# A two-block transformer kernel: the first conditioning quarter in two groups, X read first, three blocks open at once, and one reordered step of the attention stage

## What is computed

```python
mod = jax.nn.silu(c) @ w_ada[l] + b_ada[l]
shift1, scale1, gate1, shift2, scale2, gate2 = jnp.split(mod, N_MOD, axis=-1)
h = rms_norm(x, norm1_w[l]) * (1.0 + scale1[:, None]) + shift1[:, None]
proj = h @ w_in[l]
```

## Time and profile before

| | us |
|---|---|
| median of 3 runs | 2520.4 (2519.49 to 2521.88) |
| profiled execution, its own time | 2518.81 |
| span of that execution's trace, first to last instruction | 2516.9 |
| PE busy | 2475.8 (98%) |
| DVE busy | 1970.6 (78%) |
| ACT busy | 1298.0 (52%) |
| mean granted clock of PE, of full speed | 1.0 |

### The profile page before, as it was taken

How to read it: one execution, slowest core, us unless ns; L and a number is a source line. 1 busy time by engine, 2 the same in 40 slices (tenths; PEclk the granted TensorE clock), 3 DMA queues, 4 the chain that set the end, 5 groups by cost and what they waited for, 6 DMA issues and landing times.

```text
span 2516.9 us, 32571 instructions
## 1 busy us (share of the span) xinstructions
PE 2475.8 (98%) x12413; PEld 2089.9 (83%) x12413; DVE 1970.6 (78%) x2318; ACT 1298.0 (52%) x1736; POOL 258.5 (10%) x304
## 2 busy tenths in 40 slices
PE   6999999999999999999999999999999999999999
PEld 5877888878988888888888888888888888888887
DVE  7888988897888998999977687896865566665555
ACT  4544555344554544544545676566554454453553
POOL 1000310000011211111110002452000010010000
PEclk9999999999999999999999999999999999999999
DMA  9998879997899999999967656464576776766654
GB/s 348 339 353 315 290 258 328 369 320 235 297 334 340 324 341 337 322 343 335 339 231 233 184 168 193 148 220 165 192 222 233 233 224 234 226 226 198 188 191 159
DMA packets 299485, 662.87 MB, mean 263 GB/s; under 512 B 20785, under 2 KB 21137, under 8 KB 298561
## 3 DMA queue, kind: packets, MB, share of 16 engines
q1 hardware_dynamic: 296944, 652.31, 76.3%
q0 software_dynamic: 1808, 6.77, 0.8%
q10 hardware_dynamic: 576, 1.70, 0.2%
HBM read 658.61 MB, written 2.10 MB: 263 GB/s over the span
## 4 chain that ended last, share of the span: by engine, by line
PE 78%; DVE 11%; issue 4%; ACT 3%; DMA 3%; POOL 0%; SPq 0%; ACTq 0%; DVEq 0%
PE PS L662 77%; DVE WL L1573 3%; DVE ACC L1581 2%; ACT WH L1150 2%; PE PS L665 1%; DVE UQ L1573 1%; DMA RAWX<-in_w_b_up 1%; DVE A L1967 1%; ACT EX L1150 1%; DVE SM L1584 1%; DMA RAW<-in_w_in 1%; DVE KP L1573 1%; DMA RAW<-in_w_ff 0%; DVE EX L1573 0%; DVE WX L1573 0%
## 5 line engine op out<-in xcount | busy, mean ns | idle before, releaser
L1150 ACT ACTIVATE WH<-RAW 128x1024 fp32r<-128x1024 f32 x569 | 602.1, 1059 | 687.4 <-PE PS L662 524.4
L1573 DVE TENSOR_TENSOR WL<-RAW,WH 128x1024 fp32r<-128x1024 f32 x570 | 705.5, 1239 | 316.3 <-ACT WH L1150 315.0
L662 PE MATMUL PS<-WH,AH 128*128 128x512 f32 x2052 | 809.4, 394 | 6.9 <-DVE WL L1573 3.1
L662 PE MATMUL PS<-WL,AH 128*128 128x512 f32 x2052 | 799.2, 389 | 0.0
L662 PE MATMUL PS<-WH,AL 128*128 128x512 f32 x2052 | 797.8, 390 | 0.0
L662 PE MATMUL PS<-HL,WH 128*128 128x512 f32 (+1 forms) x2176 | 642.0, 383 | 0.8 <-issue 0.6
L662 PEld LDWEIGHTS PS<-WH,AH 128*128 128x128 f32 x2052 | 385.4, 188 | 90.4 <-DVE WL L1573 7.8
L662 PEld LDWEIGHTS PS<-WH,AL 128*128 128x128 f32 x2052 | 385.1, 188 | 81.2 <-DVE AL L1573 0.3
L662 PEld LDWEIGHTS PS<-WL,AH 128*128 128x128 f32 x2052 | 385.6, 188 | 76.7
L662 PEld LDWEIGHTS PS<-HL,WL 128*128 128x128 f32 x2048 | 378.3, 188 | 85.2
L662 PE MATMUL PS<-HL,WL 128*128 128x256 f32 x2048 | 397.7, 278 | 0.0
(11 more groups left out here) (250 smaller groups left out, 1921.1 us busy)
## 6 DMA issues: line engine op xcount, KB each, us to landing
RAW<-in_w_ff SPq DMA_DIRECT2D x334, 512.0 KB, 4.5
RAW<-in_w_ada SPq DMA_DIRECT2D x276, 512.0 KB, 5.3
RAW<-in_w_in SPq DMA_DIRECT2D x194, 512.0 KB, 4.4
RAWX<-in_w_ada SPq DMA_DIRECT2D x108, 512.0 KB, 5.4
RAWY<-in_w_ff SPq DMA_DIRECT2D x96, 512.0 KB, 3.7
RAWX<-in_w_ff SPq DMA_DIRECT2D x82, 512.0 KB, 5.2
RAWX<-in_w_in SPq DMA_DIRECT2D x46, 512.0 KB, 5.2
RAW<-in_w_out SPq DMA_DIRECT2D x32, 512.0 KB, 3.6
```

The source lines that it names most:

```text
L662: return e.matmul(o, l, r, start=start, stop=stop, skip_group_check=True)
L1150: return e.activation(o, i, f, **kw)
L1573: return e.tensor_tensor(o, a, b, op)
```

## The change

1. **Two groups.** The first quarter is cut in two groups of channel tiles, 0 and 1, then 2 and 3. A group is 8 items of a new kind "h": two of the 16 columns of silu(c) at once, 256 channels of shift1 and of scale1 for each. An item is two DMAs with runs of 1 KB (before, one with runs of 2 KB), and DVE accumulates it in two dependent steps over 512 columns.
2. **Order of the stream.** X, the first group, three chunks, the second group, then chunk 3 and on; the second quarter is spread over 17 chunks instead of 20.
3. **Three blocks open.** The first six chunks go in the order (0, 2, 4, 1, 3, 5): channel tiles 0 and 1 of blocks 0, 1, 2, then tiles 2 and 3 of the same. Blocks 1 and 2 are now open for four chunks each.
4. **Turns.** PE does four turns of X ahead of the first sums; turns 4 and 5 after the second sums, ahead of chunk 3; turn 6 ahead of chunk 5 and turn 7 ahead of chunk 6, in banks 6 and 7. ACT copies them at its steps 2, 6 and 7.
5. **Orders.** DVE does 8 items, the first modulation, WL and AL for it, WL of two more chunks, then the 8 items of the second group, its modulation, WL of chunk 3 and AL. keep_on is 4 and 12 products around the first sums (before 10 and 9), and 5 between turns 4 and 5.
6. **Attention ahead of rotary.** In DVE's `side`, dilated stands before rope.

```diff
+HEAD_FIRST = (0, 2, 4, 1, 3, 5)
 def sum_parts(q):
-    return ((0, 1), (1, 4)) if q == 0 else ((0, 4),)
+    return ((0, 2), (2, 4)) if q == 0 else ((0, 4),)
...
+    early = [[("h", (part, m), v[:, 2 * m:2 * m + 2, 0:2, part * 256:(part + 1) * 256]) for m in range(8)] for part in range(2)]
...
-    plan += quarter[0]
+    head = [head[c] for c in HEAD_FIRST] + head[6:]
+    plan += early[0] + head[:3] + early[1]
...
-        a, n = 20 * (q - 1), 20
+        a, n = (3, 17) if q == 1 else (20 * (q - 1), 20)
...
-            out.append(("in1" if c1 == 8 else "part", n, at, c1 - c0))
+            first, ticks = (at // 2, 4) if at in (2, 4) else (at, c1 - c0)
+            out.append(("in1" if c1 == 8 else "part", n, first, ticks))
...
-                if i == 1:
+                if i == 0:
                     e.dma_start(X[:, :, :], I["x"][0].rearrange("(t p) d -> p t d", p=128)).then_inc(s_x, 16)
...
+                if kind == "h":
+                    dst = dst.rearrange("p (t g n) -> p t g n", t=2, g=2)
+                    for t in range(2):
+                        e.dma_start(dst[:, t], src[:, t]).then_inc(s_raw[st.slot[i]], 16)
+                    continue
...
-            for i in range(8):
-                b = 4 + i % 3
+            def first_turn(i):
+                b = 4 + i % 3 if i < 4 else 6 + i % 2
...
+                if i == 5:
+                    e.wait_ge(s_mod, 6)
+                elif i > 2:
+                    e.wait_ge(s_xT, (1, 3, 0, 5, 6)[i - 3])
...
+            for i in range(4):
+                first_turn(i)
+            def early(part):
+                k0, k1 = sum_parts(0)[part]
+                e.wait_ge(s_ada, st.group_last["q", 0, part][1])
+                for k in range(k0, k1):
+                    for g in range(2):
+                        at = 512 * part + 256 * g + 128 * (k - k0)
+                        m = mm(PS[:, 7, 4 * g + k:4 * g + k + 1], ACC[:, at:at + 128], ones[:, 0:1], True, True)
+                m.then_inc(s_sum, 1)
...
             for j in range(AUP):
                 if j == 0:
-                    keep_on(3, 10)
-                if j in SUMS:
+                    keep_on(3, 4)
+                    early(0)
+                    keep_on(3, 12)
+                elif j in SUMS:
                     quarter(SUMS.index(j))
-                if j == 0:
-                    keep_on(3, 9)
+                if j == 3:
+                    early(1)
+                    first_turn(4)
+                    e.wait_ge(s_mod, 6)
+                    keep_on(7, 5)
+                    first_turn(5)
+                if j in (5, 6):
+                    first_turn(j + 1)
...
                 if j == 0:
                     feed(0)
-                    for k0, k1 in sum_parts(0):
-                        quarter(0, k0, k1)
+                    quarter(0, 0, 2)
                 if j not in norms:
                     feed(j + look(j))
+                if j == 1:
+                    quarter(0, 2, 4)
+                if j == 2:
+                    first_copy(4)
+                    first_copy(5)
+                if j in (6, 7):
+                    first_copy(j)
...
+                    if m == 0:
+                        if part == 0:
+                            e.wait_ge(s_cs, 2)
+                        ts(acc, row[:, 0, :], CS[:, 0:1], None, ALU.mult, None).then_inc(s_ada, 1)
+                    else:
+                        e.wait_ge(s_ada, st.ada[i] - 2)
+                        stt(acc, row[:, 0, :], CS[:, 2 * m:2 * m + 1], acc, ALU.mult, ALU.add).then_inc(s_ada, 1)
+                    e.wait_ge(s_ada, st.ada[i] - 1)
+                    stt(acc, row[:, 1, :], CS[:, 2 * m + 1:2 * m + 2], acc, ALU.mult, ALU.add).then_inc(s_ada, 1)
...
+                for h, s in due(p, DIL0, 8, 2, (2, 4)):
+                    dilated(h, s)
                 for r, s in due(j, ROPE0, 8, 4, (0, 4)):
                     rope(r, s)
-                for h, s in due(p, DIL0, 8, 2, (2, 4)):
-                    dilated(h, s)
...
-            for i in range(5):
+            for i in range(3):
                 item(i)
...
-            for i in range(5, 7):
+            for i in range(3, 5):
                 item(i)
...
-            for i in range(7, 16):
+            for i in range(5, 8):
                 item(i)
...
                     quarter(0)
                     feed(0)
-                    quarter_low(0, 0, 1)
+                    quarter_low(0, 0, 2)
...
+                    if j == 1:
+                        while done[0] < st.group_last["q", 0, 1][0]:
+                            item(done[0])
+                            done[0] += 1
+                        quarter(0, (1,))
                     feed(j + ahead(j))
+                    if j == 1:
+                        quarter_low(0, 1, 2)
```

More of the change, by code:

```diff
@@ L233, in __init__ @@
             age[s] = i
-            uses[s] += 1
+            uses[s] += 2 if kind == "h" else 1
             self.slot[i], self.land[i], self.before[i] = s, 16 * uses[s], held[s]
@@ L241, in __init__ @@
             else:
-                ada += 1
+                ada += 2 if kind == "h" else 1
                 self.ada[i] = ada
@@ L249, in __init__ @@
                     self.group_last["q", info[0]] = (j - 1, ada)
+                if kind == "h" and info[1] == 7:
+                    self.group_last["q", 0, info[0]] = (i + 1, ada)
         self.raw_x_done = [max([self.j[i] + 1 for i in range(n) if self.slot[i] > 3 and self.j[i] < 434
@@ L361, in __init__ @@
         for n, c0, c1 in PIECES:
-            q = self.first if n == 0 else self.starts[len(self.head)]
+            at = len(self.head)
+            q = self.first if n == 0 else self.starts[at // 2 if at in (2, 4) else at]
             self.head += [(q, c, c == c0 and (n > 0 or c == 0), c == c1 - 1) for c in range(c0, c1)]
+        self.head = [self.head[c] for c in HEAD_FIRST] + self.head[6:]
     def both(self, q):
@@ L647, in _ @@
                 dst = raw_at(i)
-                if kind != "a":
+                if kind == "h":
[3 more added lines that the diff above has]
+                    continue
+                elif kind != "a":
                     dst = dst.rearrange("p (t n) -> p t n", t=2)
@@ L758, in _ @@
                     e.wait_ge(s_dg, 2)
-                if i > 2:
-                    e.wait_ge(s_xT, i - 2)
+                if i == 5:
+                    e.wait_ge(s_mod, 6)
+                elif i > 2:
+                    e.wait_ge(s_xT, (1, 3, 0, 5, 6)[i - 3])
                 for k in (2 * i, 2 * i + 1):
@@ L771, in quarter @@
                 e.wait_ge(s_xT, 8)
[L772 to L786, removed]
+                e.wait_ge(s_mod, 3 * summed(q, 0) - 3)
+                for g in range(2):
+                    for k in range(4):
+                        at = 1024 * (q % 2) + 512 * g + 128 * k
+                        m = turn(PS[:, 6 + g, 128 * k:128 * k + 128], ACC[:, at:at + 128])
+                m.then_inc(s_sum, 1)
             def ada_turn(b, g, n):
@@ L1192, in _, with first_copy @@
             af(SM[:, 0:1], vc("q_norm_w"), ACT.Copy, scale=INV_SQRT).then_inc(s_vc, 1)
-            for i in range(8):
+            def first_copy(i):
                 e.wait_ge(s_xnT, i + 1)
-                af(xT[:, 2 * i:2 * i + 2, :].rearrange("p a s -> p (a s)"), PS[:, 4 + i % 3, :], ACT.Copy).then_inc(s_xT, 1)
+                b = 4 + i % 3 if i < 4 else 6 + i % 2
+                af(xT[:, 2 * i:2 * i + 2, :].rearrange("p a s -> p (a s)"), PS[:, b, :], ACT.Copy).then_inc(s_xT, 1)
+            for i in range(4):
+                first_copy(i)
             def quarter(q, k0, k1):
-                e.wait_ge(s_mod, 3 * summed(q, 0 if q or k1 == 1 else 1))
+                e.wait_ge(s_mod, 3 * summed(q, 0 if q or k1 == 2 else 1))
                 for k in range(4 * q + k0, 4 * q + k1):
@@ L1608, in item @@
                     return
+                if kind == "h":
+                    part, m = info
+                    acc = ACC[:, 512 * part:512 * part + 512]
+                    row = raw_at(i).rearrange("p (t n) -> p t n", t=2)
+                    if m == 0:
[7 more added lines that the diff above has]
+                    stt(acc, row[:, 1, :], CS[:, 2 * m + 1:2 * m + 2], acc, ALU.mult, ALU.add).then_inc(s_ada, 1)
+                    return
                 blk, g, t, h = info
@@ L1636, in feed, with quarter @@
                     done[0] += 1
-            def quarter(q):
-                for part, (k0, k1) in enumerate(sum_parts(q)):
+            def quarter(q, parts=(0,)):
+                for part in parts:
+                    k0, k1 = sum_parts(q)[part]
                     cols_q = slice(4 * q + k0, 4 * q + k1)
@@ L1648, in quarter @@
                             continue
-                        tt(MOD[:, row, cols_q], PS[:, 6 + (k0 > 0), 4 * g + k0:4 * g + k1], bias, ALU.add).then_inc(s_mod, 1)
```

(5 more changed lines are left out.)

## The result

The changed kernel took **2527.49 us** (median of 10 runs, 2525.96 to 2530.06) against 2519.42 for the kernel before (10 runs, 2517.22 to 2521.88): ratio **1.0032**, 95% interval 1.0024 to 1.0040. It is slower by some 8 us. The prediction was 2528.0, in a range of 2523 to 2531.5. The profiled execution took 2527.05 us; its span is 2525.2, against 2516.9 before: 8.3 more.

What follows compares the result with a forecast made beforehand. PE bounds the kernel, busy 2475.8 of 2516.9 us, so only its pauses move. Terms 7.2 + 1.8 + 0.75 - 2.3 = +7.5 us on the profiled 2518.8 give 2526.3, median 2528; range 2523 to 2531.5.

Steps and rivals of the forecast that it cites:

- First group: Start of the kernel: first turn at 20.35 us, modulation at 28.7, chunk 0 at 31.45, 6.4 us earlier than before.
- Narrower accumulation: DVE's conditioning items: two dependent 512-column steps, 0.85 us each with the gap, make a group of eight take 13.3 us.
- Second group and pause: DVE finishes at 47.9 us, PE pauses from 39.6 to 48.0 and resumes at half rate; chunk 3 at 54.4, +7.2.
- The rival that the clock stays up: PE's pause: clock stays at 2.4 GHz, chunk 3 at 52.0, sum +5.1, 2525.5 us; chance 0.15.
- Behind it: Stream after chunk 3: turns 6 and 7 between chunks add 1.8 us, late reading of a bank 0.75.
- the late bank: Chunk 6: PE waits for the bank of block n=1, which ACT reads late; +0.75 us, ends 0 and 1.35.
- Swap: Attention ahead of rotary on DVE near 1655 us: PE's waits for KP and EX both go, -2.3 us.
- the second rival: Later stages absorb up to 4 of the 4.7 us PE waits for WL: sum +3.5, 2523.9 us; chance 0.13.

Runs made afterwards that it cites:

- keep_through: The changed kernel with 32 more keep-on products between chunk 2 and the second group's sums, filling PE's pause: 2526.30 us, ratio 1.0016.
- no_swap: The changed kernel with the old order of the rotary and attention steps restored: 2528.51 us, ratio 1.0032.
- dve_two: The changed kernel with DVE accumulating items 11 and 12 of the second group ahead of the first modulation, loads unmoved: 2528.13 us, ratio 1.0028.
- x_second: The changed kernel with X loaded behind item 0, as in the kernel before: 2528.74 us, ratio 1.0036.
- ada_moved: The changed kernel with six conditioning items moved from chunks 96 to 108 of the stream to chunks 50 to 76: 2526.73 us, ratio 1.0034.
- combo2: The changed kernel with two second-group items loaded and accumulated early, turns 4 to 7 and keep-on products in PE's pause: 2522.11 us, ratio 1.0009.
- turns_in_pause: The changed kernel with turns 4 to 7 and ACT's copies of them moved into PE's pause behind chunk 2: 2524.24 us, ratio 1.0016.

## Why the prediction was right

- **First group: right.** ACT began on X at 9.92 (predicted 9.6), the first turn was at 20.69 (20.35), the first modulation at 28.85 (28.7), chunk 0 at 31.28 (31.45), the idle time of DVE there.
- **Narrower accumulation: right to 4%.** The step of 512 columns took 0.75 us, eight took 6.46, or 0.82 from start to start (predicted 0.74 and 0.85). The group took 12.8 us, predicted 13.3. The Trainium skill, VectorE: DVE Perf Modes, section The DRAIN you can't avoid, says that a semaphore after each step of a chain costs nothing extra; the estimate that I worked out from that was 11.5. These rows show 0.07 us between dependent steps and speak against 11.5. Whether the semaphore makes the gap is not shown: no run has the chain without it.
- **Second group and pause: right.** 34.64 to 47.41 (34.65 to 47.9), chunk 3 at 54.08 (54.4), **+6.9** (+7.2). The rival that the clock stays up fell: 0.50 from 43.1 on, and keep_through prices it at 2.8 us (the forecast's 54.4 less the rival's 52.0 is 2.4).
- **Behind it: slightly low.** Chunk 8 lies 2.8 us further back than chunk 3, predicted 2.55. Two turns took 0.8 and 0.9; the late bank 0.9 to 1.0 (0.75), by the mechanism forecast: on ACT the bank's reading (64.97) stands behind WH of chunk 8 (63.53) and the copy of turn 6 (64.49).
- **Swap: the term that was mis-sized.** The step that failed is "now they come 2.5 us sooner and both waits go", with "the step between has 5 us to spare". The rotary step does; but DVE's own list does not. In the changed kernel no idle time of DVE is noted from 1657 to 1692 us, and what the rotary step no longer delays for one head it delays for the next: of 2.3 us of waits 1.7 came back. Measured: -0.6 of waits, -0.3 to -0.5 from the HG pause to the end, and an interval of -4.0 to +0.5 us for the run. The prediction named the other end, 0, "another wait takes over", and took -2.3. I looked at the wait that goes and at who needs the moved step, not at what stands behind it on DVE.
- **Later stages: the second rival is not borne out.** From 9.7 us at chunk 8 the lag shrank to 8.6 by 1638 us. I had given this nothing in the forecast. The sum of PE's waits for WL is 3.4 us instead of 4.7, but 0.78 of that fall is a wait that the kernel before has at 41.60 us, ahead of chunk 3; behind chunk 8 it is 3.4 against 3.9, and 4.1 in no_swap. And no_swap, with the same start, does not repeat the fall: it is 9.5 us late at chunk 8 and 9.9 at the HG pause (1639.24). From chunk 8 to that pause the kernel before took 1568.6 us, the changed kernel 1567.4, no_swap and dve_two 1568.9, x_second 1570.0. So these 1.1 us are within what one execution differs from the next, and no gain of the later stages is shown.

In the changed kernel's trace the terms miss by -0.3 at chunk 3, +0.3 behind it, +1.7 to +2.0 by the swap and -1.1 in the later stages. That is +0.6 to +0.9 in all, as the medians (+8.1) and the spans (+8.3) have it against the forecast's +7.5. The two large misses are of opposite sign, and the second is not shown to be more than chance; the total owes some of its closeness to luck. So does the 2528.0: it counts from the earlier median of 2520.4, and beside the result the kernel before took 2519.42.

Two figures of the prediction do not come out of its own numbers. Steps with no gap between them take 1.8 us off a group (13.3 less 11.5), where the text takes 2.1 to come to +5.4; it does not say what the other 0.3 are. And nine tenths of 0.66 with half of 0.15 make 0.67, not 0.70, for slower.

## What to carry to other kernels

This start, bound by DVE, was not shortened by splitting DVE's work, since DVE then had to wait in the middle for what the first half set off. Where work is split like this, count the engine's idle time, and look whether both its order and the order of the loads let it go on. A pause of PE is to be priced with the half rate behind it (here 7.7 us and 2.8 more). A wait that is removed on an engine without idle time can come back at that engine's next deadline, as 1.7 of 2.3 us did here: look for its idle time behind the edit before the wait is booked as gained.

## What the runs showed that I had not expected

Short pauses inside the stream brought the clock down too. Behind the 1.79 us of ada_moved the mean granted clock was 0.61 over 4.40 us, behind the 2.06 us of combo2 0.56 over 3.90. Not every one did: behind the 1.69 us in turns_in_pause it was 1.00. What a mean of 0.61 over 4.40 us takes away is 0.39 x 4.40, some 1.7 us of work at full rate, an estimate; 0.44 x 3.90 gives the same. So such a wait costs nearly twice what it shows. In ada_moved the stretch with the wait became 3.1 us longer, a little less than the 3.5 of that estimate, and that is why moving the items gained nothing.
